# The gate row folded into w_out ahead of its split, and each out-projection piece added to x in one operation

## What is computed

```python
mod = jax.nn.silu(c) @ w_ada + b_ada
shift, scale, gate = jnp.split(mod, 3, axis=-1)
h = rmsnorm(x, g_norm) * (1.0 + scale[:, None, :]) + shift[:, None, :]
proj = h @ w_in
...
y_attn = rmsnorm(y_attn, g_attn_out) * jax.nn.silu(z_attn)
y_conv = rmsnorm(y_conv, g_conv_out) * jax.nn.silu(z_conv)
y = jnp.concatenate([y_attn, y_conv], axis=-1) @ w_out
x = x + gate[:, None, :] * y
return rmsnorm(x, g_final)
```

## Time and profile before

| | us |
|---|---|
| median of three runs | 277.91 (277.49 to 278.29) |
| the profiled execution, its own time | 278.23 |
| its span, first to last instruction | 276.4 |
| TensorE matmuls busy | 262.3 (95%) |
| VectorE busy | 206.9 (75%) |
| ScalarE busy | 136.2 (49%) |
| GpSimd busy | 113.1 (41%) |

### The profile page before, as it was taken

How to read it: one execution, slowest core, us unless ns; L and a number is a source line. 1 busy time by engine, 2 the same in 40 slices (tenths; PEclk the granted TensorE clock), 3 DMA queues, 4 the chain that set the end, 5 groups by cost and what they waited for, 6 DMA issues and landing times.

```text
span 276.4 us, 3680 instructions
## 1 busy us (share of the span) xinstructions
PE 262.3 (95%) x1278; PEld 215.0 (78%) x1278; DVE 206.9 (75%) x334; ACT 136.2 (49%) x228; POOL 113.1 (41%) x69
## 2 busy tenths in 40 slices
PE   5689999999999999999999999999999999999990
PEld 1367888888888888888888888887888888888880
DVE  4697887589999985969969675924595554896774
ACT  5676556447158545393544723546835764001342
POOL 2500000373806433075366322337667948451330
PEclk9999999999999999999999999999999999999998
DMA  5999963596812561119573111632832535500024
GB/s 196 361 418 415 414 256 105 197 349 180 246 68 88 155 167 62 63 68 338 184 176 100 58 70 76 154 76 77 262 120 76 199 106 171 210 0 2 38 115 152
DMA packets 12212, 45.38 MB, mean 164 GB/s; under 512 B 2081, under 2 KB 2593, under 8 KB 10786
## 3 DMA queue, kind: packets, MB, share of 16 engines
q1 hardware_dynamic: 11906, 44.89, 47.7%
q10 hardware_dynamic: 288, 0.26, 0.3%
HBM read 38.85 MB, written 2.10 MB: 148 GB/s over the span
## 4 chain that ended last, share of the span: by engine, by line
PE 90%; ACT 2%; DMA 2%; issue 2%; SPq 1%; POOL 0%; DVE 0%; POOLq 0%
PE ps L1017 22%; PE ps L1019 21%; PE ps L1018 21%; PE ps L1077 5%; PE ps L1162 4%; PE ps L1152 3%; PE ps L1140 3%; DMA xt<-in_x 2%; PE ps L1092 2%; PE ps L1098 2%; PE ps L1090 2%; PE ps L1096 2%; PE ps L1051 1%; ACT x_junk L313 1%; PE ps L1085 1%
## 5 line engine op out<-in xcount | busy, mean ns | idle before, releaser
L590 POOL TENSOR_TENSOR w_lo<-raw,w_hi 128x1024 fp32r<-128x1024 f32 x29 | 74.5, 2582 | 111.4 <-ACT w_hi L334 72.0
L1017 PE MATMUL ps<-h_lo,w_hi 128*128 128x512 f32 x200 | 79.2, 396 | 0.0
L1019 PE MATMUL ps<-h_hi,w_hi 128*128 128x512 f32 x200 | 78.0, 390 | 0.0
L1018 PE MATMUL ps<-h_hi,w_lo 128*128 128x512 f32 x200 | 78.0, 390 | 0.0
L1019 PEld LDWEIGHTS ps<-h_hi,w_hi 128*128 128x128 f32 x200 | 37.5, 188 | 7.9
L1017 PEld LDWEIGHTS ps<-h_lo,w_hi 128*128 128x128 f32 x200 | 37.5, 188 | 7.9
L1018 PEld LDWEIGHTS ps<-h_hi,w_lo 128*128 128x128 f32 x200 | 37.6, 188 | 7.5
L334 ACT ACTIVATE w_hi<-raw 128x1024 fp32r<-128x1024 f32 x29 | 30.1, 1051 | 3.2 <-DMA raw<-in_wslots 3.2
L405 ACT ACTIVATE probs<-probs,rmin 128x384 f32<-128x384 f32 (+3 forms) x32 | 17.5, 550 | 14.7 <-DVE rmin L824 14.7
L712 DVE CUSTOM_DVE_ANT_0 mod_junk<-ada,c_bc,prm 128x1024 f32<-128x1024 f32 x15 | 23.1, 1542 | 1.1
L834 DVE TENSOR_SCALAR probs<-probs,prec 128x384 f32<-128x384 f32 (+3 forms) x32 | 20.7, 709 | 0.3
(11 more groups left out here) (145 smaller groups left out, 477.1 us busy)
## 6 DMA issues: line engine op xcount, KB each, us to landing
raw<-in_wslots SPq DMA_DIRECT2D x33, 512.0 KB, 3.4
ada<-in_ada SPq DMA_DIRECT2D x11, 1024.0 KB, 8.0
raw<-in_whead SPq DMA_DIRECT2D x8, 448.0 KB, 7.3
xt<-in_x SPq DMA_DIRECT2D x4, 512.0 KB, 5.4
qd<-qt SPq DMA_DIRECT2D x16, 128.0 KB, 2.4
kd<-kt SPq DMA_DIRECT2D x16, 128.0 KB, 2.4
x<-in_x SPq DMA_DIRECT2D x4, 512.0 KB, 5.7
out<-x SPq DMA_DIRECT2D x3, 512.0 KB, 2.7
```

Source lines behind the costliest of these rows:

```text
L590: nc.gpsimd.tensor_tensor(lo, src[:, :], hi.bitcast(F32), ALU.subtract).then_inc(s_lo, 1)
L1017: nc.tensor.matmul(o, a_hi, b_lo, start=start, stop=False)
L1018: nc.tensor.matmul(o, a_lo, b_hi, start=False, stop=False)
L1019: return nc.tensor.matmul(o, a_hi, b_hi, start=False, stop=stop)
```

## The change

The gate row multiplies the raw rows of w_out on VectorE (`gate_rows(n)`, one operation of 128x1024 for each of the eight slots) before ScalarE rounds them; ScalarE's slots from 25 on wait for it. The products for slots 25 and 26 stand behind normalise(3, 1), that for 27 behind conv_gated(3), for 28 behind attn_gated(2), for 29 behind probs_low(3, 1), for 30 and 31 behind y_low(2) and y_sums(0), and for 32 behind residual(0, 1), y_sums(1) and y_low(3). A residual is one operation, PSUM times `rsy` plus x. TensorE's waits on `om_ok` become waits on `x2_ok`. The product of the last tile's left half with g_final moves behind the last reduction.

```diff
@@ scalar, slot(n)
+                if n >= W_CONV0:
+                    act.wait_ge(w_gated, n - W_CONV0 + 1)
                 nc.scalar.activation(slot_place(n)[0], src[:, :], ACT.Copy).then_inc(s_hi, 1)
@@ vector
+            def gate_rows(n):
+
+                src, arrived, count = raw_place(KT + n)
+                dve.wait_ge(arrived, count)
+                if n == W_CONV0:
+                    dve.wait_ge(gate_in, 16)
+                nc.vector.tensor_tensor(src[:, :], src[:, :], gate[:, :], ALU.mult).then_inc(w_gated, 1)
@@
             normalise(3, 1)
+            gate_rows(W_CONV0)
+            gate_rows(W_CONV0 + 1)
             probs_low(3, 0)
             conv_gated(3)
+            gate_rows(W_CONV0 + 2)
             attn_gated(2)
+            gate_rows(W_CONV0 + 3)
             join_halves(3, 0)
             probs_low(3, 1)
+            gate_rows(W_ATTN0)
             join_halves(3, 1)
             attn_gated(3)
@@ residual(g, e)
-                if i >= 2:
-                    dve.wait_ge(x2_ok, i - 1)
-                o = om[:, i % 2, 0:hi - lo]
-                nc.vector.scalar_tensor_tensor(out=o, in0=bank(b, 0, hi - lo), scalar=rsy[:, g, m:m + 1],
-                                               in1=gate[:, lo:hi], op0=ALU.mult, op1=ALU.mult).then_inc(om_ok, 1)
-                dve.wait_ge(om_ok, i + 1)
-                if i >= NC:
+                if g:
                     dve.wait_ge(x2_ok, NC)
-                nc.vector.tensor_tensor(x2[:, m, lo:hi], x2[:, m, lo:hi], o, ALU.add).then_inc(x2_ok, 1)
+                nc.vector.scalar_tensor_tensor(out=x2[:, m, lo:hi], in0=bank(b, 0, hi - lo), scalar=rsy[:, g, m:m + 1],
+                                               in1=x2[:, m, lo:hi], op0=ALU.mult, op1=ALU.add).then_inc(x2_ok, 1)
 
             for p in range(3):
                 y_low(p)
+            gate_rows(W_ATTN0 + 1)
             y_sums(0)
+            gate_rows(W_ATTN0 + 2)
             for e in range(NC):
                 residual(0, e)
                 if e == 1:
                     y_sums(1)
                     y_low(3)
+                    gate_rows(W_ATTN0 + 3)
@@
-                if e == 7:
-                    dve.wait_ge(x2_sq, 7)
-                    nc.vector.tensor_tensor(x2[:, 3, 0:BANK], x2[:, 3, 0:BANK], gfin[:, 0:BANK], ALU.mult
-                                            ).then_inc(x2_left, 1)
...
-            dve.tensor_tensor_reduce(om[:, 1, 0:hi - lo], x2[:, m, lo:hi], x2[:, m, lo:hi], 1.0 / D, ss2[:, 12:13], ALU.mult,
+            dve.tensor_tensor_reduce(sum_junk[:, 0:hi - lo], x2[:, m, lo:hi], x2[:, m, lo:hi], 1.0 / D, ss2[:, 12:13], ALU.mult,
                                      ALU.add, fin_e[:, m:m + 1]).then_inc(fin_sum, 1)
+
+            dve.wait_ge(x2_sq, 7)
+            nc.vector.tensor_tensor(x2[:, m, 0:BANK], x2[:, m, 0:BANK], gfin[:, 0:BANK], ALU.mult).then_inc(x2_left, 1)
             dve.wait_ge(fin_rs, TT)
@@ tensor
-            pe.wait_ge(om_ok, 2)
+            pe.wait_ge(x2_ok, 2)
...
-                pe.wait_ge(om_ok, e + 1)
+                pe.wait_ge(x2_ok, e + 1)
```

More of the change, by code:

```diff
@@ L111, in build @@
         kd = sb("kd", [2, S], F32R)
-        om = at("om", base, [2, BANK])
+        sum_junk = at("sum_junk", base, [BANK])
         base = cursor[0]
@@ L193, in build @@
         y_hi, yc_low_ok, ya_low_ok = sem("y_hi"), sem("yc_low_ok"), sem("ya_low_ok")
-        gate_out, gate_in = sem("gate_out"), sem("gate_in")
-        acc_out, om_ok, x2_ok, x2_sq, x2_g = [sem("acc_conv"), sem("acc_attn")], sem("om_ok"), sem("x2_ok"), sem("x2_sq"), sem("x2_g")
+        gate_out, gate_in, w_gated = sem("gate_out"), sem("gate_in"), sem("w_gated")
+        acc_out, x2_ok, x2_sq, x2_g = [sem("acc_conv"), sem("acc_attn")], sem("x2_ok"), sem("x2_sq"), sem("x2_g")
         part_ok, x2_left = sem("part_ok"), sem("x2_left")
@@ L951, in residual @@
                 dve.wait_ge(acc_out[g], e + 1)
-                if i == 0:
-                    dve.wait_ge(gate_in, 16)
                 if g == 0 and e % 2 == 0:
```

## The result

| | before | after |
|---|---|---|
| median | 278.17 us (7 runs) | 280.14 us (7 runs, 278.88 to 281.02) |
| ratio | | 1.0074, 95% interval 1.0055 to 1.0093 |
| the profiled execution, its own time | 278.23 us | 279.30 us |
| its span | 276.4 us | 277.5 us |

The change is slower by 2.0 us. That is inside the range (277.3 to 281.0) and on the side held likeliest, but 1.4 us above the forecast of 278.75. The profiled execution alone shows +1.1 us. So there are two questions: whether the +1.1 is made as forecast, and where the rest of the median's +2.0 comes from.

What follows compares the result with a forecast made beforehand. TensorE, 90% of the chain that ended last, and the 7.2 us behind its last matmul were taken to bound the kernel. Stall +1.82 less tail 0.98 gave +0.84 on the median 277.91: 278.75 us, range 277.3 to 281.0.

Steps and rivals of the forecast that it cites:

- the side held likeliest: Sign of the whole change: slower was given 0.45, the same 0.43, faster 0.12.
- the slack of 1.22 us: In front of head 7's low part: slot 28's rounding may start 1.22 us late before TensorE has to wait.
- Size of the stall: TensorE held in front of head 7's low part: 2.99 + 0.05 less the slack 1.22, 1.82 us.
- the chain: Products, splits and roundings of slots 24 to 28, step by step, until ScalarE starts slot 28 at 219.58.
- the rule: VectorE/GpSimd port: a held VectorE operation ends its length less 0.20 behind GpSimd's end; a held split 2.27 behind VectorE's.
- the forecast order: At the shared port, a waiting GpSimd operation enters when VectorE's ends; product 28 leads slot 27's split by 0.56 us.
- The place near 140 us: A split issued at 139.63 took 4.35, VectorE being let in first at 140.46; counted against the port order used.
- The rival at 280.9: Slot 27's split gets the port in front of product 28, a stall of 3.96 us; chance 0.17.
- Tail: Behind TensorE's last matmul: 1.35 us from the fused residual less 0.37 for the held last power, giving 0.98.
- The 0 to 0.3 set aside for the last transfers: At the end, the last output quarters may share transfer time with tile 2's output; cost 0 to 0.3, taken as 0.
- What lies behind moves along: Behind the stall: products 29 to 32 cause no further stall; 30 and 31 lie where the first residual waits for x.
- cases of a small stall and of none: At slot 28: stall of 0.65 us from its late load, 277.6, chance 0.11; no stall, 276.9, chance 0.12.

Runs made afterwards that it cites:

- late_slots: The changed kernel with ScalarE rounding slots 27 and 28 behind the copy of the other half and head 7's probabilities' high part; 277.51 us against 277.91, ratio 0.9987.
- slot28_late: The changed kernel with only slot 28's rounding moved behind the high part of head 7's probabilities, slot 27 staying in front; 278.06 us against 277.91, ratio 1.0007.
- act_pause: The kernel before with five idle 128x512 copies on ScalarE in front of the copy of head 7's other half, no gate products; 280.28 us against 278.03, ratio 1.0083.
- product27_first: The changed kernel with the product for slot 27 in front of the convolution's gated product on VectorE; 282.92 us against 277.89, ratio 1.0167.
- products_only: The kernel before with only the eight gate products and ScalarE's waits for them added, so the gate is applied twice; 280.17 us against 277.91, ratio 1.0091.
- product_back: The changed kernel with the product with g_final put back in front of the last small sum; 279.21 us against 277.89, ratio 1.0058.
- The second measurement: The changed kernel measured again without any edit, beside the kernel before; 279.33 us against 277.89, ratio 1.0050.

## Why the prediction was right, and where not

**Direction and main mechanism: right.** ScalarE's order, the slack of 1.22 us and the port decided, as forecast: late_slots takes the stall away, slot28_late leaves 0.31 of it, act_pause makes it without a product.

**Size of the stall: 1.82 forecast, 2.09 measured.** Of the chain, product 28 was put at 218.32 to 219.54, which is 218.24 to 219.46 in the changed trace, where all is 0.08 earlier; it ran 218.45 to 219.66, 0.2 late. The main term that was short is the hand-over from VectorE's wide product to ScalarE, taken at 0.04 and measured at 0.12 (219.66 to 219.78). It stands in the chain twice, at slots 25 and 28, and makes 0.16 of the 0.27; most of the rest is two held products (25 and 27), which each ended 0.06 to 0.07 later behind their split than the rule says. Behind what released it, each split and each held product fell where the rule put it, within 0.1 us. The 0.05 that the sum adds to 2.99 has no row behind it; the traces have 0.04 there.

**Order at the port: the forecast order.** GpSimd's waiting split went before product 27, and product 28 before slot 27's split, issued 0.67 us behind it at 219.12. In this stretch the order is that of issue. The Trainium skill's page SBUF — State Buffer, section Who interferes with whom, describes the shared port pair as a lock that is held for a whole instruction; the runs agree, with four ends of product27_first within 0.1 us of that. The place near 140 us stays against it: it is in the changed kernel too (a split issued at 139.53 that takes 4.35), and no run here explains it. The rival at 280.9 did not occur; product27_first shows what such an order looks like. By the time alone one would have taken it: 280.14 lies nearer to 280.9 than to 278.75, and only the list of waits and product 28's place tell them apart.

**Tail: 0.98 forecast, 0.96 measured.** The power beside the moved product took 0.93 (forecast 0.54 + 0.37 = 0.91), from the one row of the statistics' power at 238.50. What the prediction did not say is that the move then gives nothing: it should have worked out the tail without the move as well. The 0 to 0.3 set aside for the last transfers did not appear: the span grew by 1.11 and the execution's own time by 1.07.

**What lies behind moves along: right for the changed kernel, wrong as a general claim.** Products 30 and 31 were costed at nothing because the first residual waits for x. But TensorE too waits for the statistics, at the fourth piece, and that was in time only because of the stall. With the stall gone it is the next thing that is late (0.87 us of the stream in slot28_late). The prediction's cases of a small stall and of none, 277.6 and 276.9, were too fast for that reason: late_slots, which has no stall, measured 277.51.

**The forecast itself: 278.75 against 280.14.** The term that is missing is the granted clock. The sum priced a stall at its length. In 6 of 19 runs of the changed kernel the mean clock was low and the run took 1.2 to 1.6 more; the traces of products_only and product_back show such a run with the clock at half for 3.4 us. The prediction had no case for this; the trace of before could not show it, since TensorE never pauses there between the head and the end. Of the 1.39 between forecast and median, 0.26 is the kernel before itself, whose median was 278.17 beside the changed kernel and 277.91 when the forecast was made, 0.27 is the stall and the tail (+1.11 in the traces in place of +0.84), and the other 0.9 is what the low runs do to the median. At full clock the changed kernel is 1.2 to 1.3 us slower, close to the traces' +1.11. That the first median still fell inside the range is partly luck: its upper bound of 281.0 was set for GpSimd in front of product 28, and not for a lower clock. The second measurement, 279.33, lies within 0.6 of the forecast.

## What to carry to other kernels

When work is put on an engine that has room, read what stands behind its consumer on every in-order queue: here VectorE had room for eight products, and the early ones cost 2 us because ScalarE's rounding of their results stood in front of something TensorE needed. Where a VectorE operation with two SBUF inputs meets a GpSimd operation that reads SBUF, lay the two out one behind the other, whole instructions at a time, as all such rows around 210 to 222 us do; the low part of head 7, with one input in PSUM, ran its 1.49 us beside a split without delay. The order then says more than the lengths, and moving a product forward can cost more than it wins (product27_first). Price a new pause of TensorE above its length, and take the next wait behind it into the sum before you say what removing it gives.

## What the hardware showed that was not expected

- The granted clock fell to half for 3.4 us right behind two pauses of 1.0 and 0.7 us in the profiled executions of products_only and product_back, and not in three profiled executions with such a pair of pauses (the changed kernel twice, and act_pause, whose first pause is 0.8). By the mean clock, 11 of 38 runs of these four kernels had it. With a pause of 3.1 us all four runs were low, and in the profiled one the clock was at half for 6.8 us from inside the pause on.
- A power of one column (128x1) on GpSimd, 0.54 alone, took 0.93 beside a VectorE product with two SBUF inputs that was issued 0.16 us earlier, in each of the seven traces that have this pair at the end.
- ScalarE started 0.12 us behind the end of the 128x1024 product of VectorE that it waited for (four slots of the changed kernel, 0.115 to 0.116).
